# A two-layer decoder trunk: GpSimd takes over the low parts of the last three output-projection pieces, and the index mask is written in three steps

## The chip, the cores and the metric

The kernel runs on one core of one Trainium2 chip. The metric is the device time of one execution in microseconds (us), lower is better; the median of the runs is compared. Engines are named as the profile names them: PE is TensorE (matrix products), DVE is VectorE, ACT is ScalarE, POOL is GpSimd, SP is the engine that issues most transfers (DMA).

## What is computed

Two layers, each a token mixer and a mixture of experts, on 256 tokens of width 1024 in float32. The parts that matter here:

```python
p = _split_columns(x @ w_in)              # one input projection, 11 pieces of 256 columns
o_fox = _fox_attention(...)               # 4 heads
o_nsa = _nsa_attention(...)               # 6 heads: compressed + selected + window branches
o_dsa = _dsa_attention(...)               # 6 heads, keys picked by an index score:
#   score = where(pos_k <= pos_q, score, NEG); idx = top_k(score, 64)
o = jnp.concatenate([o_fox, o_nsa, o_dsa], axis=-1)
x = _layer_norm(ALPHA * x + o @ w_out)    # output projection, 4 pieces of 256 columns
x = _layer_norm(ALPHA * x + _moe(x))      # 64 experts, top 8, and one shared expert
```

## The kernel before, in words

Each engine has its own program, written out by hand, and the engines wait for each other on semaphores; what stands in one engine's program runs in that order. The two layers run the same code. Per layer there is an attention stage (some 160 us in layer 0, with the output projection, the layer norm and the routing) and an expert stage (some 460 us), in which the expert weights stream in.

**Weights in two parts.** Most products of the mixer are done three times, as high part by high part, low by high and high by low. A projection piece (128 partitions x 8 blocks x 256 columns, 2048 elements per partition) lies in one of five slots, `piece[n % 5]`. Its high part `piece_hi` is the piece rounded (`split_hi`, on ACT, L1244 to L1247; there are four slots for high parts). Its low part `piece_lo` is the piece minus its high part, written over the piece itself. Two engines share the low parts: the numbers in `LO_VECTOR` (L38) are done by DVE, with one instruction of 2048 elements (`split_lo`, L1634) or with two halves of 1024 (`split_out`, L1738); the others (`LO_POOL`) by POOL, with eight instructions of 256 elements (`split_lo`, L1488 to L1494). The pieces are numbered in the order in which they arrive: 9 to 12 are the last four input pieces, 13 to 16 the four output pieces.

**The attention units.** There are eleven units u = 0 to 10, two heads each (`UNITS`: fox 0 and 1, then selected and window alternating for u = 2 to 7, then dsa for 8 to 10). A unit goes through four engines: PE makes the scores (`scores(u)`); DVE takes the maxima (`maxima(u)`, L1668); ACT makes the exponentials (`exps(u)`, L1307); DVE divides by the sums (`normalise(u)`: a reciprocal L1678, for u = 2 to 7 a product with the gates L1681, two products over `prob` L1685); PE turns the result (`turn_probs`, L778); ACT copies it out (`probs_out`, L1325); PE multiplies it with the values (`add_values`, L802). The first five units are laid between the last input projection tiles (`project_tile`), with the rotation of the heads (`rotate`, L1560 to L1566) on DVE. The others run in a loop on each engine, in which PE does `scores(u + 2)`, `turn_probs` of u, and `add_values` of the turn before; DVE does `normalise(u)`, `maxima(u + 2)`; ACT does `exps(u + 1)`, `probs_out` of u and, for some, `heads_out` (L1317).

**The output projection.** It follows with 96 products. Its first parts are done early (`out_early`, between the last units): those need the low parts of pieces 13 and 14 and the first four heads in two parts (`heads_split` of 4). Those head parts, `x_hi` and `x_lo`, are made by POOL (L1509, L1510) for seven heads and by DVE (L1765, L1766) for the eighth, one head at a time as ACT delivers them. The next early part needs pieces 15 and 16.

**Index mask.** `index_top` marks the 64 best keys per query in `score` (128 x 384). `index_mask` (L1613) turns the marks into an additive mask `dmask` in bf16, which PE adds to the scores of the dsa units, 8 to 10.

SP's program issues the layer-norm rows, router and shared weights when the eighth head is out (`o_sb` of 8, L531 to L535), and the first expert weights when the output projection is nearly done (`mix`, L536).

## Time and profile before

| | us |
|---|---|
| median of 3 runs | 1241.99 (1241.19 to 1243.54) |
| profiled execution, whole time | 1243.89 |
| its span, first to last instruction | 1242.1 |
| PE busy | 1209.8 (97%) |
| DVE busy | 555.9 (45%) |
| ACT busy | 340.2 (27%) |
| POOL busy | 122.9 (10%) |

The page's chain that ended last goes through PE for 79% of the span, DVE 11%, DMA 6%, ACT 2%. Busy shares over the whole span say little about the attention stage, so that stage is read from the waits and the order of time. The two attention stages lie at 0 to 161 us and at 624 to 776 us. Where text below says layer 0 and layer 1, these are meant.

### The profile page before, as it was taken

Reading aid. Unit: us, or ns where it says so; the run is one execution under the profiler, and the core shown is the slowest. Engines: PE = TensorE matmul, PEld = TensorE weight load, DVE = VectorE, ACT = ScalarE, POOL = GpSimd, SP = SyncE. Lnnn points to the kernel's source line nnn. Section 1 sums busy time; section 2 is a strip of 40 time slices with the busy share of each in tenths; the row PEclk is TensorE's granted clock in tenths of the full one; section 3 lists DMA queues with packets and bytes.
Section 4 is the critical chain, followed back from the end, with each engine's and each line's share of the span. In section 5 each row is a group of like instructions: output and inputs, shape, how many; then the busy total and the mean of one; then the engine's idle time right before and its main releaser. Section 6 shows DMA issues by size and latency. Waiting matters only on the chain.

```text
span 1242.1 us, 25211 instructions
## 1 busy us (share of the span) xinstructions
PE 1209.8 (97%) x10381; PEld 631.4 (51%) x10383; DVE 555.9 (45%) x1550; ACT 340.2 (27%) x701; POOL 122.9 (10%) x173
## 2 busy tenths in 40 slices
PE   9998999999999999999999989999999999999995
PEld 7885754334344443433398858433433444443341
DVE  4788553333333333333468877433333333333334
ACT  4667321111111111111265574111111111111111
POOL 2662110000000000000035421000000000000000
PEclk9999999999999999999999999999999999999998
DMA  9444799999999999999945529999999999999994
GB/s 356 166 178 206 281 399 427 425 426 427 425 425 424 429 426 426 426 426 426 385 149 190 222 99 360 389 427 426 425 428 425 427 424 427 425 427 426 425 427 189
DMA packets 42425, 454.88 MB, mean 366 GB/s; under 512 B 4944, under 2 KB 5712, under 8 KB 8016
## 3 DMA queue, kind: packets, MB, share of 16 engines
q1 hardware_dynamic: 42032, 452.27, 87.6%
q8 instruction: 85, 1.39, 0.5%
q10 hardware_dynamic: 288, 1.05, 0.2%
q14 instruction: 20, 0.16, 0.0%
HBM read 452.26 MB, written 1.05 MB: 365 GB/s over the span
## 4 chain that ended last, share of the span: by engine, by line
PE 79%; DVE 11%; DMA 6%; ACT 2%; issue 2%; DVEq 0%; POOL 0%; ACTq 0%; POOLq 0%
PE banks L1050 33%; PE banks L1070 17%; PE banks L1026 7%; PE banks L1081 5%; DMA expert_weights<-in_moe_w 5%; PE banks L1058 2%; PE banks L970 1%; PE banks L917 1%; DVE prob L1685 1%; PE banks L918 1%; PE banks L919 1%; PE banks L633 1%; PE banks L1007 1%; PE banks L601 1%; DVE sm_neg L1668 1%
## 5 line engine op out<-in xcount | busy, mean ns | idle before, releaser
L1050 PE MATMUL banks<-expert_weights,gathered 128*64 128x512 f32 x1520 | 339.8, 595 | 1.4 <-DMA expert_weights<-in_moe_w 1.4
L1050 PEld LDWEIGHTS banks<-expert_weights,gathered 128*64 128x64 f32 x1520 | 105.6, 137 | 230.7 <-issue 230.7
L1070 PE MATMUL banks<-expert_weights,hT 128*32 128x512 f32 x1600 | 182.0, 595 | 2.5 <-DVE hT L1892 2.5
L1887 DVE TENSOR_TENSOR sig<-sig,banks 128x256 f32<-128x256 f32 x64 | 27.0, 421 | 338.9 <-ACT sig L1422 338.6
L1435 ACT ACTIVATE y_hi<-banks,gate_slot 128x512 fp32r<-128x512 f32 x126 | 86.6, 687 | 295.1 <-PE banks L1070 295.1
L1897 DVE SCALAR_TENSOR_TENSOR y_lo<-banks,gate_slot,y_hi 128x512 fp32r<-128x512 f32 x126 | 94.6, 751 | 157.4 <-ACT y_hi L1435 157.4
L1422 ACT ACTIVATE sig<-banks 128x256 f32<-128x256 f32 x64 | 24.6, 384 | 407.8 <-PE banks L1050 407.8
L1026 PEld LDWEIGHTS banks<-hot,x_part 128*128 128x128 bf16 x3072 | 93.3, 98 | 48.7 <-issue 48.7
L1070 PEld LDWEIGHTS banks<-expert_weights,hT 128*32 128x32 f32 x1600 | 47.2, 109 | 109.7 <-issue 108.2
L1026 PE MATMUL banks<-hot,x_part 128*128 128x64 bf16 x3072 | 100.7, 193 | 0.0
L1491 POOL TENSOR_TENSOR piece_lo<-piece,piece_hi 128x256 fp32r<-128x256 f32 x112 | 87.8, 819 | 80.3 <-ACT piece_hi L1247 65.2
L601 PE MATMUL banks<-piece_hi,x_hi 128*128 128x256 f32 x224 | 66.1, 295 | 0.0
L602 PE MATMUL banks<-piece_lo,x_hi 128*128 128x256 f32 x224 | 63.8, 285 | 0.0
L603 PE MATMUL banks<-piece_hi,x_lo 128*128 128x256 f32 x224 | 63.7, 285 | 0.0
L1050 PE MATMUL banks<-expert_weights_in_ring,gathered 128*64 128x512 f32 x256 | 58.1, 596 | 0.2 <-DMA expert_weights_in_ring<-in_moe_w 0.2
L1081 PE MATMUL banks<-y_hi,hotT 64*128 64x512 f32 x252 | 56.5, 444 | 0.1
L1247 ACT CAST piece_hi<-piece 128x2048 fp32r<-128x2048 f32 x24 | 45.6, 1903 | 22.2 <-DMA piece<-in_pieces 21.3
L1081 PE MATMUL banks<-y_lo,hotT 64*128 64x512 f32 x252 | 49.9, 391 | 0.0
L1873 DVE COPY gathered<-banks 128x512 f32<-128x512 f32 x64 | 44.3, 692 | 12.3 <-PE banks L1026 12.2
L1537 POOL TENSOR_TENSOR shared_hT<-shared_sig,shared_hT 128x512 f32<-128x512 f32 x2 | 2.6, 1282 | 477.0 <-ACT shared_hT L1444 477.0
L1426 ACT COPY gathered<-banks 128x512 f32<-128x512 f32 x64 | 37.5, 586 | 25.8 <-PE banks L1026 25.6
L601 PEld LDWEIGHTS banks<-piece_hi,x_hi 128*128 128x128 f32 x224 | 43.4, 194 | 1.1 <-issue 0.8
(244 smaller groups left out, 1526.0 us busy)
## 6 DMA issues: line engine op xcount, KB each, us to landing
expert_weights<-in_moe_w SPq DMA_DIRECT2D x132, 2048.0 KB, 23.2
expert_weights_in_ring<-in_moe_w SPq DMA_DIRECT2D x20, 2048.0 KB, 23.3
piece<-in_pieces SPq DMA_DIRECT2D x32, 1024.0 KB, 5.0
expert_weights<-in_moe_w SPq DMA_DIRECT2D x26, 1024.0 KB, 8.2
expert_weights_in_rows<-in_moe_w SPq DMA_DIRECT2D x22, 1024.0 KB, 22.5
expert_weights_in_x<-in_moe_w SPq DMA_DIRECT2D x22, 1024.0 KB, 23.3
expert_weights_in_ring<-in_moe_w SPq DMA_DIRECT2D x8, 1024.0 KB, 7.8
shared_weights<-in_ws SPq DMA_DIRECT2D x2, 3072.0 KB, 12.8
```

What stands on the lines that cost most here:

```text
L601: pe.matmul(out_, x_hi[:, k, cols], hi[:, k, :], start=(k == 0 and opens), stop=False, skip_group_check=True)
L602: pe.matmul(out_, x_hi[:, k, cols], lo[:, k, :], start=False, stop=False, skip_group_check=True)
L603: mm = pe.matmul(out_, x_lo[:, k, cols], hi[:, k, :], start=False, stop=(k == KD - 1), skip_group_check=True)
L1026: mm = pe.matmul(o[:, :, t, :], xs[j][t][:, d * P:(d + 1) * P], H[:, t, :, :], start=(j == 0), stop=(j == 2))
L1050: mm = pe.matmul(C[e * PAIR:(e + 1) * PAIR, :], xgT[:, d, e * PAIR:(e + 1) * PAIR], w[e][:, part], start=(d == 0), stop=(d == KD - 1))
L1070: mm = pe.matmul((A, B)[c][to:to + SLOTS, :], hT[:, f, of_:of_ + SLOTS], W[QUARTERS + c][e][:, f * 512:(f + 1) * 512], start=(f == 0), sto ...
L1081: mm = pe.matmul(bank[2 * t + c][:, :], hotT[par][rows_, :], y[rows_, c * 512:(c + 1) * 512], start=False, stop=False, skip_group_check=True)
L1247: act.copy(flat_piece(hi_of(n)), flat_piece(piece[n % RING])).then_inc(hi_ready, 1)
L1435: act.activation(y_hi[:, c * 512:(c + 1) * 512], (A, B)[c][:, :], ACT.Copy, scale=gslot[:, par:par + 1]).then_inc(sw.yh, 1)
L1491: own.mark(G.tensor_tensor(piece_lo[n % RING][:, k, :], piece[n % RING][:, k, :], hi_of(n)[:, k, :].bitcast(F32), ALU.subtract))
L1873: V.tensor_copy(xgT[:, 4:8, :], B[:, :].rearrange("p (k c) -> p k c", k=4)).then_inc(sw.xg_dve, 1)
L1897: V.scalar_tensor_tensor(y_lo[:, c * 512:(c + 1) * 512], (A, B)[c][:, :], gslot[:, par:par + 1], y_hi[:, c * 512:(c + 1) * 512].bitcast(F3 ...
```

## The change

It has three parts.

- **Low parts.** Pieces 14, 15 and 16 leave `LO_VECTOR`; DVE's `split_lo(14)` and its four halves `split_out` are gone. POOL makes them, after the compressed values (`vc_blocks`) and before the first head parts, eight instructions of 256 elements each.
- **High part of piece 16.** ACT's two half pieces (`split_last_hi`, L1249) are gone. POOL makes this one too, with eight copies of 256 elements, once the last input projection is done; `hi_ready` counts one less.
- **Index mask.** Before: one comparison over 384 columns, two additions of the causal mask over 128 columns, one cast over 384. Now: two comparisons over 128 columns in place, one that writes the middle 128 columns of `dmask` directly, and two minima of score and causal mask that write the outer 128 columns. `dmask_ready` counts to 3. Beside it, `masks_ready` takes the place of `heads_known` in layer 0.

```diff
-LO_VECTOR = (2, 3, 6, 14, 15, 16)
+LO_VECTOR = (2, 3, 6)
...
-        dmask_ready = sem("dsa_mask_ready", 1)
+        dmask_ready = sem("dsa_mask_ready", 3)
...
                     probs_out(4)
-                    split_last_hi(0)
                     read_turned(10)
...
                         heads_out(v - 1)
-                        if v == 6:
-                            split_last_hi(1)
...
                     if layer == 0:
-                        pool.wait_ge(heads_known, 1)
+                        pool.wait_ge(masks_ready, 1)
...
+                    for n in SPLIT_OUT[1:3]:
+                        rounded_by_scalar(n)
+                        split_lo(n)
+                    n = SPLIT_OUT[3]
+                    pool.wait_ge(*at(piece_ld[n % RING], piece_count(n)))
+                    hi_free(pool, n)
+                    for k in range(KD):
+                        own.mark(G.tensor_copy(hi_of(n)[:, k, :], piece[n % RING][:, k, :]))
+                    own.settle()
+                    split_lo(n)
                     pool.wait_ge(*at(proj, 2 * N_IN_PIECES))
                     pool.wait_ge(*at(m_ready, 6))
...
                     def index_mask():
-                        own.link(V.tensor_scalar(score[:, :], score[:, :], -2.0e38, NEG, ALU.is_gt, ALU.mult))
                         for a in (0, 2 * P):
-                            own.mark(V.tensor_tensor(score[:, a:a + P], score[:, a:a + P], cmask[:, 0, :], ALU.add))
+                            own.mark(V.tensor_scalar(score[:, a:a + P], score[:, a:a + P], -2.0e38, NEG, ALU.is_gt, ALU.mult))
+                        V.tensor_scalar(dmask[:, P:2 * P], score[:, P:2 * P], -2.0e38, NEG, ALU.is_gt, ALU.mult).then_inc(dmask_ready, 1)
                         own.settle()
-                        V.tensor_copy(dmask[:, :], score[:, :]).then_inc(dmask_ready, 1)
+                        for a in (0, 2 * P):
+                            V.tensor_tensor(dmask[:, a:a + P], score[:, a:a + P], cmask[:, 0, :], ALU.min).then_inc(dmask_ready, 1)
...
                     rotate(8)
                     index_mask()
-                    split_lo(14)
...
                         normalise(u)
-                        if 5 <= u < 9:
-                            split_out(2 + (u - 5) // 2, (u - 5) % 2)
-                        if u in (6, 8):
-                            own.settle()
-                            dve.nop().then_inc(lo_dve, 1)
```

POOL, from the low parts of pieces 12 and 13 to the first head, before (the number behind `piece_` is that of a slot: 57 holds piece 13, 58 piece 14, 54 piece 15, 55 piece 16):

```order
L1491 TENSOR_TENSOR piece_lo<-piece_56,piece_hi 128x256 x8
L1491 TENSOR_TENSOR piece_lo<-piece_57,piece_hi 128x256 x8
L1503 TENSOR_TENSOR vc_blocks<-vc_sb,own_head 96x384
L1509 CAST x_hi<-xT 128x256
L1510 TENSOR_TENSOR x_lo<-xT,x_hi 128x256
```

The same place of POOL after the change:

```order
L1477 TENSOR_TENSOR piece_lo<-piece_56,piece_hi 128x256 x8
L1477 TENSOR_TENSOR piece_lo<-piece_57,piece_hi 128x256 x8
L1494 TENSOR_TENSOR vc_blocks<-vc_sb,own_head 96x384
L1477 TENSOR_TENSOR piece_lo<-piece_58,piece_hi 128x256 x8
L1477 TENSOR_TENSOR piece_lo<-piece_54,piece_hi 128x256 x8
L1503 CAST piece_hi<-piece_55 128x256 x8
L1477 TENSOR_TENSOR piece_lo<-piece_55,piece_hi 128x256 x8
L1510 CAST x_hi<-xT 128x256
L1511 TENSOR_TENSOR x_lo<-xT,x_hi 128x256
```

Thirty-two instructions have come in between the compressed values and the first head.

DVE in the unit loop, units 5 and 6, before:

```order
L1678 RECIPROCAL sm_r<-sm_sum 128x4
L1681 TENSOR_TENSOR sm_r<-sm_r,gates 128x4
L1685 TENSOR_TENSOR prob<-prob,sm_r 128x2x128
L1685 TENSOR_TENSOR prob<-prob,sm_r 128x2x256
L1741 TENSOR_TENSOR piece_lo<-piece_54,piece_hi 128x1024
L1668 TENSOR_REDUCE sm_neg<-banks 128x2 x2
```

The same place of DVE after the change:

```order
L1680 RECIPROCAL sm_r<-sm_sum 128x4
L1683 TENSOR_TENSOR sm_r<-sm_r,gates 128x4
L1687 TENSOR_TENSOR prob<-prob,sm_r 128x2x128
L1687 TENSOR_TENSOR prob<-prob,sm_r 128x2x256
L1670 TENSOR_REDUCE sm_neg<-banks 128x2 x2
```

The half piece between the products over `prob` and the maxima has gone, in four units of each layer.

## Rows read from the trace of the kernel before

**Rows 1.** PE's waits, 64 to 135 us: us in total, times, longest
```profile
PE banks L778 <- DVEq L1687: 3.5, 4, 1.1
```

**Rows 2.** PE's waits, 679 to 750 us
```profile
PE banks L778 <- DVEq L1687: 3.6, 4, 1.3
```

**Rows 3.** PE in order of time: start, us, instruction, idle before and its releaser
```profile
89.07 0.44 PE L653 MATMUL banks<-ident,hq 128*128 128x128 f32 x2 [0.46 <-DVEq L1567]
...
120.15 0.84 PE L778 MATMUL banks<-ident,prob 128*128 128x128 f32 x6 [1.06 <-DVEq L1687]
...
703.06 0.69 PE L653 MATMUL banks<-ident,hq 128*128 128x128 f32 x2 [1.00 <-DVEq L1567]
...
735.56 0.85 PE L778 MATMUL banks<-ident,prob 128*128 128x128 f32 x6 [0.76 <-DVEq L1687]
```

**Rows 4.** Busy time by stretch: stretch, length, PE, PEld, DVE, ACT, POOL, PEclk, DMA, GB/s
```profile
702.60:706.10 3.50, 3.04 (x14) 2.96 (x14) 3.07 (x12) 2.79 (x8) 2.45 (x4) 0.51 1.03 433
```

**Rows 5.** DVE in order of time, the mask and piece 14, layer 0
```profile
79.28 0.67 DVE L1614 TENSOR_SCALAR score<-score 128x384 f32<-128x384 f32 x1
...
82.18 2.28 DVE L1636 TENSOR_TENSOR piece_lo<-piece,piece_hi 128x2048 fp32r<-128x2048 f32 x1
```

**Rows 6.** All instructions on tile piece_lo, two of its groups: ns min/median/max
```profile
L1491 POOL TENSOR_TENSOR piece_lo<-piece,piece_hi x112: 716/737/2828, 24.4 to 703.5; 128x256 fp32r<-128x256 f32 x112
...
L1741 DVE TENSOR_TENSOR piece_lo<-piece,piece_hi x8: 1224/1225/1528, 107.8 to 735.5; 128x1024 fp32r<-128x1024 f32 x8
```

**Rows 7.** POOL in order of time, layer 0, low parts of 12 and 13, then head parts
```profile
75.82 6.23 POOL L1491 TENSOR_TENSOR piece_lo<-piece,piece_hi 128x256 fp32r<-128x256 f32 x8 [8.23 <-DVEq L1687]
82.23 8.01 POOL L1491 TENSOR_TENSOR piece_lo<-piece,piece_hi 128x256 fp32r<-128x256 f32 x8 [0.18 <-POOL piece_lo L1491]
90.48 0.82 POOL L1503 TENSOR_TENSOR vc_blocks<-vc_sb,own_head 96x384 f32<-96x384 f32 x1 [0.24 <-POOL piece_lo L1491]
...
115.48 1.05 POOL L1510 TENSOR_TENSOR x_lo<-xT,x_hi 128x256 fp32r<-128x256 f32 x1
```

**Rows 8.** DVE, the same instructions with POOL idle and with POOL at work
```profile
74.66 1.02 DVE L1685 TENSOR_TENSOR prob<-prob,sm_r 128x256 f32<-128x256 f32 x2
...
101.63 0.17 DVE L1681 TENSOR_TENSOR sm_r<-sm_r,gates 128x4 f32<-128x4 f32 x1
...
106.13 0.45 DVE L1681 TENSOR_TENSOR sm_r<-sm_r,gates 128x4 f32<-128x4 f32 x1
...
680.14 1.94 DVE L1685 TENSOR_TENSOR prob<-prob,sm_r 128x256 f32<-128x256 f32 x2
```

**Rows 9.** DVE in order of time, from the compressed scores to unit 5, both layers
```profile
89.10 0.54 DVE L1720 TENSOR_TENSOR pc<-banks,misc_c 128x45 f32<-128x45 f32 x4
...
99.87 0.42 DVE L1560 TENSOR_TENSOR hq<-banks,rope_cs 128x256 f32<-128x256 f32 x1 [0.71 <-PE banks L603]
...
101.42 0.18 DVE L1678 RECIPROCAL sm_r<-sm_sum 128x4 f32<-128x4 f32 x1
...
103.00 2.19 DVE L1668 TENSOR_REDUCE sm_neg<-banks 128x2 f32<-128x256 f32 x4
...
707.46 1.02 DVE L1668 TENSOR_REDUCE sm_neg<-banks 128x2 f32<-128x256 f32 x2 [1.15 <-PE banks L760]
...
715.20 0.42 DVE L1560 TENSOR_TENSOR hq<-banks,rope_cs 128x256 f32<-128x256 f32 x1 [1.05 <-PE banks L603]
```

**Rows 10.** ACT in order of time: exponentials of unit 5, copy out, half piece
```profile
104.11 0.37 ACT L1307 ACTIVATE prob<-banks,sm_neg 128x128 f32<-128x128 f32 x1 [0.41 <-DVEq L1670]
...
106.01 0.80 ACT L1325 COPY probT<-banks 128x768 f32<-128x768 f32 x1 [0.17 <-ACT prob L1307]
...
110.34 1.04 ACT L1253 CAST piece_hi<-piece 128x1024 fp32r<-128x1024 f32 x1 [0.17 <-ACT probT L1325]
...
719.44 0.37 ACT L1307 ACTIVATE prob<-banks,sm_neg 128x128 f32<-128x128 f32 x1 [0.41 <-DVEq L1670]
```

**Rows 11.** The queue of SP: the first transfer after the attention units
```profile
130.44 0.33 SPq L532 DMA_DIRECT2D ln_rows<-in_lnw  x1
```

More of the change, by code:

```diff
@@ L1247, in split_hi @@
                         act.copy(flat_piece(hi_of(n)), flat_piece(piece[n % RING])).then_inc(hi_ready, 1)
-                    def split_last_hi(half):
-                        n, cols = SPLIT_OUT[3], slice(half * SLOT // 8, (half + 1) * SLOT // 8)
-                        act.wait_ge(*at(piece_ld[n % RING], piece_count(n)))
-                        hi_free(act, n)
-                        own.mark(act.copy(flat_piece(hi_of(n))[:, cols], flat_piece(piece[n % RING])[:, cols]))
-                        if half:
-                            own.settle()
-                            act.nop().then_inc(hi_ready, 1)
                     if layer == 0:
```

21 lines of the change are left out of this document (8 added, 13 removed).

## Prediction

> **What bounds the kernel now.** I looked for the stage in which DVE, ACT and POOL work can be on the path at all. The change touches only the attention stage, so I read PE's waits there first: between 64 and 135 us PE waits 3.5 us in four times for the end of `normalise` on DVE [rows 1], and in layer 1 3.6 us in four times [rows 2]. Beside these it waits once per layer for a rotated head, 0.46 us and 1.00 us [rows 3]. Where PE does not wait it is fed, so these waits are about all that a faster DVE can give back, unless the waits also change PE's clock.
>
> That they do, once: in layer 1, from 702.6 to 706.1 us, the granted clock is 0.51, so PE is at the lower of its two levels (1.2 GHz) [rows 4]; this begins in the 1.00 us for which PE stood idle before 703.06. In layer 0 the same place has an idle time of 0.46 us.
>
> After the attention units nothing else changes order, and later work hangs on their end: SP issues its first transfer after them at 130.44 us, when the eighth head is out [rows 11]. The expert stream starts behind that, so I pass on a shift of the attention stage one for one.
>
> **The change, part by part.**
>
> *Piece 14 and the mask.* DVE loses one instruction of 2.28 us at 82.18 [rows 5]. Behind it stand the rotation of a head and, at 89.10, the compressed scores [rows 9], for which DVE waits on PE. So only PE's 0.46 us (layer 0) and 1.00 us (layer 1) come back; the rest of the 2.28 us becomes idle time on DVE. In layer 1 the half-speed stretch should go too. The mask took 2.9 us from 79.28 to 82.18, with POOL at work [rows 5]: four instructions. Now it is five shorter ones, of which four or five meet POOL; I put it at 2.5 to 3.5 us. Since 2.28 us of idle time lie behind it and its reader is unit 8, some 30 us later, it costs nothing.
>
> *What POOL's work does to DVE.* This is the main term. POOL's instructions of 256 elements take 0.737 us in the median, but one took 2.828 us [rows 6], and one group of eight took 8.01 us instead of 6.23 [rows 7]: it stood beside DVE's 2.28 us instruction, so the two do not run at once. It goes the other way too: the pair of products over `prob` takes 1.02 us with POOL idle and 1.94 us with POOL at work, and the product with the gates 0.17 and 0.45 us [rows 8]. Each two-input DVE instruction waits for the running POOL instruction to end. That makes 0.92 + 0.28 = 1.2 us on a `normalise` of units 2 to 7, and 0.92 us on the others. Rotations, maxima and other reads of PSUM don't meet it.
>
> The Trainium skill says the same (GPSIMD Engine Reference, Key points): GpSimd shares its SBUF interfaces with VectorE, and contention is with instructions that have two SBUF inputs or run in a two-port mode. It speaks against this change, and the rows agree; it gives no price, and the sum goes by the rows.
>
> When does POOL now work? It ended `vc_blocks` at 91.3 us [rows 7]. Without DVE's 2.28 us lock-out this comes at about 89.4. Then two groups at 6.23 us, eight casts at about 0.4 each (my estimate, from half to all of the 0.737 us of a subtraction: 3 to 6 us), and a third group at 6.23: POOL is at work until about 112 us, where before it stood idle between 91.3 and the first head part, at about 104.
>
> *From 89 us to the exponentials of unit 5.* In this stretch DVE does `normalise` 2, 3 and 4, now each beside POOL: 3 x 1.2 = 3.6 us. One rotation and the four small products and subtractions of the compressed branch meet it also, at 0.1 to 0.45 us each; I take 1.0 together. Sum 4.6 us. Against it stands DVE's own idle time: in layer 0, 0.71 us [rows 9] and some 0.3 us in small waits, together 1.0, and the start that is 0.4 earlier (PE's wait gone). So unit 5's exponentials, which started at 104.11 on a wait for DVE [rows 10], come 4.6 - 1.0 - 0.4 = 3.2 us later. In layer 1 DVE idled 1.15 and 1.05 us [rows 9] and about 0.4 more, because PE ran slowly: 2.6 us, so 4.6 - 2.6 - 0.4 = 1.6 us later. PE's clock stretch and its 1.00 us are inside this, so they are not counted again.
>
> *From there to the turn of unit 8.* Before: from 104.11 to 120.15 [rows 3, 10] 16.04 us, and in layer 1 from 719.44 to 735.56 [rows 3, 10] 16.12 us. On DVE four half pieces go, 4 x 1.225 = 4.9 us and up to 5.2 with the slowest one [rows 6], and on ACT one half piece of 1.04 us [rows 10]; ACT's other one stood before a wait for DVE, and gives nothing. What is late next? DVE without them: 1.9 us of exponentials, four times 1.58 us of `normalise` (101.42 to 103.00 [rows 9]) and three times 1.17 us of maxima (1.02 and the step to the next), 11.7 us. ACT: exponentials 1.90 (104.11 to 106.01), copy 0.97 and a head copy 0.3 are some 3.1 us for each unit [rows 10]; three of them, then 1.9 and 1.6 us, are 12.8 us. So ACT's pace would hold, at 12.8. But POOL is still at work until 112, and then makes up for three heads: `normalise` 5 and 6 meet it fully and 7 in part, 2.4 to 3.6 us on DVE, 14.1 to 15.3 us. Some of it overlaps with ACT's pace; I take 14.5. The gain is 16.1 - 14.5 = 1.6 us in each layer.
>
> *Sum.* Layer 0: +3.2 - 1.6 = +1.6 us. Layer 1: +1.6 - 1.6 = 0. With 0.2 us for the casts that the last two units may still meet: **+1.8 us**. The profiled execution took 1243.89 us, 1.9 more than the median of 1241.99; a shift applies to both, so it would be 1245.7, and the median **1243.8 us**.
>
> **Ends of the range.** If POOL's work cost DVE nothing, unit 5 would come 0.5 us earlier in layer 0 and 2.3 in layer 1 (1.00 and some 1.3 us of slow clock), and the second stretch would be 12.8: -3.8 and -5.6, together -9.4 us, 1232.6. If every listed instruction paid the full 0.7 us of a POOL instruction, the first stretch would be some 2.4 us longer and the second 15.3: +3.2 us more in each layer, 1250.2. Both are further than the 8 in 10.
>
> **The rivals.**
>
> *Contention at half price (faster).* A DVE instruction is held only if it comes while a POOL instruction runs, and POOL may itself be held by DVE so often that both meet less. With 2.3 us in place of 4.6 in the first stretch and 13.5 in the second, layer 0 gives +0.9 - 2.6 = -1.7 and layer 1 -0.7 - 2.6 = -3.3: -5.0 us, 1237.0. For it: the product with the gates at 106.13 pays 0.28 us and not a whole POOL instruction of 0.737 [rows 6, 8]. Against it: where POOL works back to back, as now for over 20 us, the one pair in the trace paid in full. Chance 0.22.
>
> *The waits cost clock as well (slower).* PE's clock fell beside an idle time of 1.00 us. Now PE waits over 1 us for `normalise` 4, 5 and perhaps 6. Its idle times of up to 1.1 us in layer 0 [rows 1] did not bring the clock down, so this is open. One stretch like that of rows 4 costs some 1.3 us; one in each layer, on the forecast: +1.8 + 2.6 = +4.4 us, 1246.4. It decides from +0.7 us above the forecast on. The same sign comes if contention is a third above my price (+3 us). Chance 0.35.
>
> *POOL becomes the bound (slower).* It is done with piece 16 at about 112 us, then needs 1.2 to 1.7 us for each of four heads: 117 to 119. PE asks for the fourth head at about 122 to 124, so 3 us are left. Only with all three groups at 8.01 us would this be gone: then +1.8 and about 2 more, 1246. Chance 0.03, within the slower case.
>
> **How the numbers follow.** Forecast +1.8 us, within 0.2% (2.5 us, about what a measurement can tell from no change): 0.42. Half price or less: 0.22, which is faster. Slow clock, dearer contention or POOL as the bound: 0.36, slower. The range is 1237.5 to 1248.0: it takes in half price and one slow stretch in each layer with some contention above them. The likeliest case alone would be 1241.5 to 1245.
>
> **What would show it.** Right: `prob` pairs of units 2 to 5 at 1.7 to 1.95 us; POOL busy without a gap from 89 to 112 us; unit 5's exponentials near 107.3 in layer 0; the time from there to unit 8's turn near 14.5; no granted clock of 0.5 around 703 us. Wrong: pairs at 1.0 beside POOL (then it is faster), PE waiting for head parts L1511 or for the low parts of 15 and 16 before its early products (then POOL is the bound), or new half-speed stretches between 104 and 120 us.

## The result

The changed kernel takes 1248.60 us (median of five runs, 1246.85 to 1249.81), the kernel before, timed beside it, 1242.91 us: ratio 1.0046, 95% interval 1.0035 to 1.0057. It is 5.7 us slower, where +1.8 us was forecast, and lies 0.6 us above the range. Timed once more, beside new runs of the kernel before, the same kernel took 1247.46 us against 1242.25, ratio 1.0039 (1.0026 to 1.0052).

The profiled execution took 1248.61 us, with a span of 1246.7 us, 4.6 us more than that of before. Where they arise is read from three marks in each layer: the transfer of a piece by SP before the attention units, the first exponential of unit 5 on ACT, and SP's first transfer after the units. Three rows of SP's queue in the kernel after (both marks of layer 0, the last of layer 1), and two of ACT. The piece of layer 1 was issued at 683.74 us:

```profile
76.14 0.33 SPq L478 DMA_DIRECT2D piece<-in_pieces  x1
133.12 0.33 SPq L531 DMA_DIRECT2D ln_rows<-in_lnw  x1
...
750.81 0.33 SPq L531 DMA_DIRECT2D ln_rows<-in_lnw  x1
```
```profile
106.28 0.37 ACT L1297 ACTIVATE prob<-banks,sm_neg 128x128 f32<-128x128 f32 x1 [1.09 <-DVEq L1672]
...
723.86 0.37 ACT L1297 ACTIVATE prob<-banks,sm_neg 128x128 f32<-128x128 f32 x1 [1.09 <-DVEq L1672]
```

Before, the second and third mark of layer 0 stood at 104.11 and 130.44 us [rows 10, 11]; its piece was issued at 76.85. In layer 1 the three marks stood at 680.16, 719.44 and 745.85. I call the first stretch, from the piece to unit 5, part 1, and the second, from unit 5 to SP's transfer, part 2. All differences below are taken with these two parts, so that the chance shifts at the start of a run drop out:

| execution | part 1, layer 0 | part 2, layer 0 | part 1, layer 1 | part 2, layer 1 | PE at half speed in part 2 (layers 0, 1) |
|---|---|---|---|---|---|
| before | 27.26 | 26.32 | 39.28 | 26.41 | none (3.4 us in part 1 of layer 1) |
| after | 30.14 | 26.84 | 40.12 | 26.95 | 6.8, 6.8 us |
| after minus before | +2.9 | +0.5 | +0.8 | +0.5 | |
| forecast | +3.2 | -1.6 | +1.6 | -1.6 | |

Part 1 came out as worked out in layer 0, and below it in layer 1. The gain of part 2 is missing in both. The rest of the program moves by less than 1 us.

PE's waits between 64 and 135 us (us in total, times, longest), against [rows 1]: the waits for `normalise` are as long in total, but one of them is now 2.0 us, and those for ACT have grown from 1.2 to 2.3 us. The first two lines are of the kernel after, the third is of the kernel before.

```profile
PE banks L777 <- DVEq L1689: 3.4, 3, 2.0
PE banks L661 <- ACTq L1300: 2.3, 3, 1.3
```
```profile
PE banks L662 <- ACTq L1310: 1.2, 2, 0.8
```

In order of time, PE in both layers:

```profile
108.10 0.93 PE L661 MATMUL banks<-qkT 64*128 64x128 f32 x8 [1.34 <-ACTq L1300]
111.32 1.51 PE L777 MATMUL banks<-ident,prob 128*128 128x128 f32 x6 [1.97 <-DVEq L1689]
...
122.81 0.85 PE L777 MATMUL banks<-ident,prob 128*128 128x128 f32 x6
```
```profile
725.67 0.93 PE L661 MATMUL banks<-qkT 64*128 64x128 f32 x8 [1.34 <-ACTq L1300]
728.90 1.51 PE L777 MATMUL banks<-ident,prob 128*128 128x128 f32 x6 [1.98 <-DVEq L1689]
...
740.50 0.84 PE L777 MATMUL banks<-ident,prob 128*128 128x128 f32 x6
```

From unit 5's exponentials to the turn of unit 8 this is 16.53 us (122.81 less 106.28) and in layer 1 16.64, where the prediction had 14.5 and the kernel before 16.04 and 16.12.

The six transposes take 1.51 us behind the wait of 1.97 us and 0.85 us eleven microseconds later. The busy time by stretch (the columns of [rows 4]) says why: the granted clock is 0.51 for 6.9 us in each layer, so PE is at 1.2 GHz there. The stretch begins inside the wait, and in the 5.9 us before it (the third line, layer 0) the clock was at 1.00.

```profile
109.90:116.80 6.90, 5.48 (x26) 3.56 (x27) 4.92 (x9) 3.80 (x16) 4.12 (x7) 0.51 0.01 4
727.70:734.60 6.90, 5.70 (x27) 3.78 (x28) 4.92 (x8) 3.48 (x15) 3.90 (x7) 0.51 0.00 0
104.00:109.90 5.90, 4.01 (x32) 2.48 (x31) 4.82 (x9) 4.10 (x15) 5.82 (x9) 1.00 0.59 244
```

DVE in order of time, the `prob` products of units 2 to 6 and one subtraction of the compressed branch, and POOL from the low part of piece 14 on:

```profile
88.62 1.10 DVE L1726 TENSOR_TENSOR pc<-pc,pcs 128x90 f32<-128x90 f32 x2
...
90.37 2.08 DVE L1687 TENSOR_TENSOR prob<-prob,sm_r 128x256 f32<-128x256 f32 x2
...
96.23 2.04 DVE L1687 TENSOR_TENSOR prob<-prob,sm_r 128x256 f32<-128x256 f32 x2
...
103.69 1.33 DVE L1687 TENSOR_TENSOR prob<-prob,sm_r 128x256 f32<-128x256 f32 x2
...
109.08 2.04 DVE L1687 TENSOR_TENSOR prob<-prob,sm_r 128x256 f32<-128x256 f32 x2
```
```profile
88.17 6.24 POOL L1477 TENSOR_TENSOR piece_lo<-piece,piece_hi 128x256 fp32r<-128x256 f32 x8
94.59 6.46 POOL L1477 TENSOR_TENSOR piece_lo<-piece,piece_hi 128x256 fp32r<-128x256 f32 x8 [0.18 <-POOL piece_lo L1477]
101.28 3.19 POOL L1503 CAST piece_hi<-piece 128x256 fp32r<-128x256 f32 x8 [0.24 <-POOL piece_lo L1477]
104.56 6.01 POOL L1477 TENSOR_TENSOR piece_lo<-piece,piece_hi 128x256 fp32r<-128x256 f32 x8
110.83 0.55 POOL L1510 CAST x_hi<-xT 128x256 fp32r<-128x256 f32 x1 [0.26 <-POOL piece_lo L1477]
```

POOL is busy from 88 to 110.6 us, as worked out, and a pair of products costs 2.04 to 2.08 us beside its subtractions, a little above the 1.94 of [rows 8], and 1.33 beside its casts.

Behind unit 6 something else is new: DVE now waits for PE's scores before it can take the maxima, 1.62 and 0.90 us in layer 0 and 1.62 and 1.02 us in layer 1. Before, no maxima of this part waited over 0.3 us for them.

```profile
116.69 1.02 DVE L1670 TENSOR_REDUCE sm_neg<-banks 128x2 f32<-128x256 f32 x2 [1.62 <-PE banks L756]
...
120.20 1.02 DVE L1670 TENSOR_REDUCE sm_neg<-banks 128x2 f32<-128x256 f32 x2 [0.90 <-PE banks L756]
```

### The profile page after: what moved, and what is told of

Same layout as the page of the kernel before. It is cut to its first block, busy times and chain, and to the rows that moved or that the text cites. A ratio compares the mean times of both kernels' runs of the same rounds, so it can differ in the third digit from the quotient of the medians.

```text
span 1246.7 us, 25263 instructions
## 1 busy us (share of the span) xinstructions
PE 1212.5 (97%) x10383; PEld 633.4 (51%) x10383; DVE 554.3 (44%) x1542; ACT 336.3 (27%) x697; POOL 158.5 (13%) x237
## 3 DMA queue, kind: packets, MB, share of 16 engines
q10 hardware_dynamic: 288, 1.05, 0.2%
HBM read 452.26 MB, written 1.05 MB: 364 GB/s over the span
## 4 chain that ended last, share of the span: by engine, by line
PE 82%; DVE 9%; DMA 6%; ACT 1%; issue 1%; DVEq 0%; ACTq 0%
PE banks L1049 33%; PE banks L1069 17%; PE banks L1025 7%; PE banks L1080 5%; DMA expert_weights<-in_moe_w 5%; PE banks L1057 1%; PE banks L600 1%; PE banks L969 1%; PE banks L602 1%; PE banks L601 1%; PE banks L916 1%; DVE prob L1687 1%; PE banks L918 1%; PE banks L917 1%; PE banks L632 1%
## 5 line engine op out<-in xcount | busy, mean ns | idle before, releaser
L1477 POOL TENSOR_TENSOR piece_lo<-piece,piece_hi 128x256 fp32r<-128x256 f32 x160 | 120.4, 787 | 79.5 <-ACT piece_hi L1246 63.7
```

What stands on the lines that cost most here:

```text
L1477: own.mark(G.tensor_tensor(piece_lo[n % RING][:, k, :], piece[n % RING][:, k, :], hi_of(n)[:, k, :].bitcast(F32), ALU.subtract))
```

## The experiments

Each was timed in five rounds or more beside the kernel before on the same chip. Most changes are given against the kernel before or the changed one.

### The mask alone

```diff
-own.link(V.tensor_scalar(score[:, :], score[:, :], -2.0e38, NEG, ALU.is_gt, ALU.mult))
+for a in (0, 2 * P):
+    own.mark(V.tensor_scalar(score[:, a:a + P], score[:, a:a + P], -2.0e38, NEG, ALU.is_gt, ALU.mult))
...
-V.tensor_copy(dmask[:, :], score[:, :]).then_inc(dmask_ready, 1)
+for a in (0, 2 * P):
+    V.tensor_tensor(dmask[:, a:a + P], score[:, a:a + P], cmask[:, 0, :], ALU.min).then_inc(dmask_ready, 1)
```

> The kernel before with the new mask alone (two thresholds, one threshold straight into the mask tile, two minima). The theory of the prediction: the mask is hidden behind DVE's later wait for PE, so no change, within 0.6 us of before. A rival, in which the mask carries part of the 5.7 us by which the changed kernel is slower (a shift of DVE's work by 0.5 to 1 us that POOL then meets at other places): +1 to +3 us.

1243.16 us against 1243.10, ratio 1.0006 (0.9995 to 1.0018): no change. DVE in order of time, the first instruction of the mask and the one behind it:

```profile
78.81 1.23 DVE L1615 TENSOR_SCALAR score<-score 128x128 f32<-128x128 f32 x2
...
81.61 2.82 DVE L1637 TENSOR_TENSOR piece_lo<-piece,piece_hi 128x2048 fp32r<-128x2048 f32 x1
```

The mask takes 2.8 us, from 78.81 to 81.61, within the 2.5 to 3.5 us given for it. PE stood idle 0.98 us for the rotated head in layer 1, as before, and here no half-speed stretch followed: part 1 of layer 1 took 37.62 us in place of 39.28. So behind a wait of 1.0 us the clock falls in some executions and not in others. The two kernels also differ in the mask, so the 1.7 us are the most that this stretch can have cost.

### What could be gained at best

```diff
-LO_VECTOR = (2, 3, 6, 14, 15, 16)
+LO_VECTOR = (2, 3, 6)
...
-                    split_lo(14)
...
-                            split_out(2 + (u - 5) // 2, (u - 5) % 2)
...
-hi, lo = hi_ring[...], lo_ring[:, first % RING:first % RING + 2]
+hi, lo = hi_ring[...], hi_ring[:, hi_slot(first):hi_slot(first) + 2]
```

> The kernel before with the low parts of pieces 14, 15 and 16 left out: neither DVE nor POOL makes them, and the output projection takes the high parts in their place, with as many products. It has neither DVE's work nor POOL's, so it bounds what the move could give at best. The prediction's bound without contention was -9.4 us with the rounding of 16 off ACT too; here ACT keeps it, about 1 us a layer, so -7 us by that working, of which 1.3 us is a half-speed stretch that goes. Rival: PE's own pace or ACT's takes over sooner, -3 us. From here to the changed kernel is then the whole price of POOL's work: 13 us by the first, 9 us by the second.

The low parts of 14, 15 and 16 are left out. 1236.79 us against 1243.10, ratio 0.9951 (0.9938 to 0.9963): -6.3 us, close to the -7. This kernel computes less than the reference asks for; it is a bound and not a candidate. Parts 1 are 0.4 and 2.7 us shorter than before, parts 2 2.2 and 2.6 us. So layer 1 gains 5.3 us, near the 5.6 of the prediction's lower end, and layer 0 2.6 us where that had 3.8 (with the rounding off ACT too). From here to the changed kernel is the whole price of doing the work on POOL, what it does to PE included: 11 to 12 us.

### Piece 14 alone, and one instruction that is passed by six

```diff
-LO_VECTOR = (2, 3, 6, 14, 15, 16)
+LO_VECTOR = (2, 3, 6, 15, 16)
...
+split_lo(LO_POOL[-1])
...
-split_lo(14)
```

> The kernel before, of which only piece 14 goes from DVE to POOL; the low parts of 15 and 16 stay on DVE, the rounding of 16 on ACT, and the mask is the old one. Theory 1 (the clock makes the loss of the changed kernel): PE's waits stay short here, since POOL is done at about 96 us; no half-speed stretch in layer 0 and none around 703 us in layer 1; 0 to -3 us, and more if a stretch of layer 1 is gone. Theory 2 (contention makes it, evenly with POOL's work): a third of POOL's new work gives a third of the loss, about +2 us, less the 1.5 us of the two waits for a rotated head, so about +0.5 us, with the clock as before.

POOL makes piece 14 behind `vc_blocks`. 1247.84 us against 1243.10, ratio 1.0040 (1.0028 to 1.0052). Both expectations miss: a third of the work gives most of the loss. But the profiled execution took 1243.11 us, and the other five 1245.8 to 1249.4. I ran it again for another profile.

> The kernel with only piece 14 on GpSimd once more, unchanged, to have a profile of another execution and more times. Theory 1 (DVE is passed in some executions): the profile shows either about 1243 us and no DVE instruction held for over 1 us, or 1246 us and more and one that was held for 3 to 5 us, most likely one of the products or subtractions of the compressed branch beside piece 14. Theory 2 (instruction loading or the clock): a gap of 2 us and more on PE that waits for nothing, or half-speed stretches.

1249.14 us against 1242.11, ratio 1.0047 (1.0033 to 1.0061), and this profile caught what was missing. DVE, POOL and PE in the second profile, layer 0:

```profile
90.12 5.22 DVE L1725 TENSOR_TENSOR pc<-pc,pcs 128x90 f32<-128x90 f32 x2
```
```profile
89.68 5.56 POOL L1491 TENSOR_TENSOR piece_lo<-piece,piece_hi 128x256 fp32r<-128x256 f32 x8
```
```profile
97.14 1.51 PE L778 MATMUL banks<-ident,prob 128*128 128x128 f32 x6 [3.52 <-DVEq L1688]
```

In the first profile the same pair on DVE read:

```profile
89.13 1.10 DVE L1725 TENSOR_TENSOR pc<-pc,pcs 128x90 f32<-128x90 f32 x2
```

The first of the two subtractions took 4.53 us in place of 0.40. It came while POOL's first instruction on piece 14 ran, and was held through that and six more, which stand end to start behind it; POOL's group was not slowed at all (5.56 us for eight). The 3.52 us for which PE then waited were followed by a half-speed stretch of 6.8 us. Part 1 took 33.21 us in place of 28.30. Theory 1 holds in this profile. (Expectations further down speak of eight instructions: that is POOL's whole group. It is the running one and six that passed.)

The Trainium skill (SBUF — State Buffer, "SBUF: two separate sides") says that of two such instructions the one that starts first keeps the ports for its whole length and the other blocks. The holds of one instruction agree with it (the pair took 1.10 us beside POOL in the first profile, and 0.42 us without POOL in the run with piece 14 begun later, below); that the one that waits may be passed by six later ones is not in the rule, and is measured here.

Two edits test it. First, POOL waits for the end of each of its instructions on pieces 12 to 14 before it issues the next:

```diff
 for k in range(KD):
     own.mark(G.tensor_tensor(...))
+    if n >= 12:
+        own.settle()
```

> The kernel with only piece 14 on GpSimd, with the same edit. That kernel's profiled execution took 1243.1 us, its other ones 1245.8 to 1249.4. Theory 1: what they have more is DVE passed by many GpSimd instructions, 3 to 5 us in one place; with the instructions apart all runs come to 1240 to 1244 us. Theory 2: the times stay at 1246 to 1249 us.

1243.65 us against 1242.11, ratio 1.0009 (1.0000 to 1.0018); eleven of twelve runs lie between 1242.8 and 1244.6. The 5 us are gone although POOL's group now takes 7.05 us. Second, the instructions end to start as they were, but begun only after DVE's subtraction:

```diff
+pool.wait_ge(*at(sc_sub, 1))
 split_lo(LO_POOL[-1])
```

> The kernel with only piece 14 on GpSimd, its eight instructions end to start as there, but begun only when DVE's subtraction in the compressed branch is done. In three kernels whose profile showed it, or didn't, the +5 us stood with that subtraction: passed by eight instructions in one execution (1249.0 us) and not in another (1243.1). Theory 1 (it is this meeting): no passing there, median 1242 to 1244.5 us in place of 1247.8 to 1249.1, without a gap between GpSimd's instructions. Theory 2 (any DVE instruction meets the same chance in a back-to-back group): passed elsewhere, median at 1246 us and more.

1243.14 us against 1242.25, ratio 1.0005 (0.9995 to 1.0015). DVE and POOL:

```profile
89.59 0.42 DVE L1726 TENSOR_TENSOR pc<-pc,pcs 128x90 f32<-128x90 f32 x2
```
```profile
90.14 6.38 POOL L1491 TENSOR_TENSOR piece_lo<-piece,piece_hi 128x256 fp32r<-128x256 f32 x8 [0.96 <-DVEq L1728]
```

So it is this one meeting: in this profile the other DVE instructions beside the same back-to-back group are held, but not passed. The edit with gaps in the kernel before, whose POOL groups are those of 12 and 13:

> The kernel before with the same edit: GpSimd's instructions on pieces 12 and 13 one at a time. The runs of the kernel before spread over 5 us (1240.4 to 1245.9). Theory 1 (in some executions DVE is passed by many GpSimd instructions): the slowest runs go, the median falls by 1 to 2 us. Theory 2 (the spread has another cause): the median and the spread stay.

1244.29 us against 1242.11, ratio 1.0012 (1.0003 to 1.0021): slightly slower, and the spread stays. Theory 1 falls for the kernel before. Its spread has another cause, which I did not find. The profile of this run has a wait of 1.70 us for the rotated head of layer 1 in place of 1.00.

### How long one hold is

```diff
-own.mark(G.tensor_tensor(piece_lo[n % RING][:, k, :], ...))
+for a in (0, P) if n >= 12 else (0,):
+    cols = slice(a, a + P) if n >= 12 else slice(0, PIECE)
+    own.mark(G.tensor_tensor(piece_lo[n % RING][:, k, cols], ...))
+    if n >= 12:
+        own.settle()
```

> The kernel with only piece 14 on GpSimd, its instructions apart, and each of them on 128 elements of a row in place of 256 (16 for a piece, pieces 12 to 14). If a DVE instruction is held until the running GpSimd instruction ends, halved ones hold it half as long: the pairs beside them fall from about 1.9 us to about 1.4, and the time by 0 to 1 us from 1243.65 (more instructions on GpSimd, each with its own start, take part of it back: a piece takes 8 us in place of 6.6). If the hold is a fixed price of each meeting: pairs as before, and up to 1 us slower.

This is the kernel with piece 14 alone, with 16 instructions of 128 elements in a piece in place of 8 of 256, one at a time. 1243.40 us, ratio 1.0017 (1.0008 to 1.0026), where the one with 8 had 1.0009 (1.0000 to 1.0018): no gain in time. But the two pairs beside POOL read, in DVE's order of time:

```profile
90.06 1.44 DVE L1690 TENSOR_TENSOR prob<-prob,sm_r 128x256 f32<-128x256 f32 x2
...
95.38 1.43 DVE L1690 TENSOR_TENSOR prob<-prob,sm_r 128x256 f32<-128x256 f32 x2
```

A pair takes 1.02 us with POOL idle [rows 8], 2.04 to 2.08 beside instructions of 256 elements end to start, and 1.57 beside the same ones apart, where only its second product is held, by 0.53 us. Here both are held, by 0.15 and 0.26 us. So a hold shortens with the POOL instruction: it is the rest of the running one and not a fixed price. But there are more of them, and with 0.1 us off a pair nothing comes out in the time.

### PE's clock in the changed kernel

```diff
+if v == 6:
+    pe.wait_ge(*at(o_sb, 2))
+    for _ in range(8):
+        pe.matmul(bank[7][:, 0:T], still[:, 0:P], still[:, 0:T], start=True, stop=True, ...)
 if what == "unit" and u + 2 < NU:
     scores(u + 2)
...
+if v in (6, 7):
+    pe.wait_ge(*at(pt_sb, v))
+    for _ in range(12 if v == 6 else 5):
+        pe.matmul(bank[5][:, 0:T], ...)
 turn_probs(v)
```

> The changed kernel, with 25 extra products of 128x256 bf16 zeros in each layer that PE makes where it otherwise stands idle around 105 to 115 us: 8 before the scores of unit 7, 12 before the turn of unit 6 and 5 before the one of unit 7. All other work and its order are those of the changed kernel. Theory 1 (half-speed stretches make the loss): both stretches of 6.8 us are gone or shorter, and the time falls by 3 to 5 us from the changed kernel's +5.7 us, to +1 to +2.5 us. Theory 2 (contention alone makes it; PE at half speed is only hidden beside waits): the stretches go, and the time stays at +5 to +6 us.

1250.45 us against 1243.10, ratio 1.0058 (1.0045 to 1.0071). The stretches are gone, and by the time alone theory 2 would stand. The profile says that the time of this run doesn't decide it, because two other things came in. Stretches, then two rows of DVE, then PE between the layers:

```profile
109.90:116.80 6.90, 5.74 (x50) 3.88 (x49) 6.21 (x12) 4.41 (x18) 4.32 (x7) 1.00 0.00 1
727.70:734.60 6.90, 5.66 (x50) 3.85 (x49) 5.79 (x10) 5.29 (x21) 6.40 (x11) 1.00 0.01 2
```
```profile
119.08 1.02 DVE L1678 TENSOR_REDUCE sm_neg<-banks 128x2 f32<-128x256 f32 x2 [1.05 <-PE banks L756]
...
706.38 5.21 DVE L1734 TENSOR_TENSOR pc<-pc,pcs 128x90 f32<-128x90 f32 x2
```
```profile
621.16 1.04 PE L821 MATMUL banks<-still 128*128 128x512 bf16 x4 [2.18 <-issue]
```

The pair of subtractions took 5.21 us in layer 1, passed as above, and PE waited 3.5 us for it. And the program, longer by 50 products, has a gap of 2.18 us on PE in which nothing that the profile shows is waited for. In part 2, where the clock was kept, it did gain: 25.54 and 25.53 us in place of 26.84 and 26.95, that is 1.3 and 1.4 us. Most of it is the wait of 1.62 us for PE's scores, which is gone; the next, for unit 9, is still 1.05 us, at full clock. From unit 5's exponentials to the turn of unit 8 it takes 15.23 us in both layers, so 0.7 us above the forecast of 14.5 stay with the clock kept.

The same with the gaps on POOL, and with 13 products of 512 columns:

```diff
+for _ in range(4):
+    pe.matmul(bank[7][:, 0:2 * T], still[:, 0:P], still[:, 0:2 * T], ...)
...
+for _ in range(6 if v == 6 else 3):
+    pe.matmul(bank[5][:, 0:2 * T], still[:, 0:P], still[:, 0:2 * T], ...)
...
+if n >= 12:
+    own.settle()
```

> The changed kernel with GpSimd's instructions one at a time, and with 13 extra products of 128x512 bf16 zeros in each layer in PE's waits around 105 to 115 us (half as many, twice as long as in the first such kernel). Theory 1 (two causes that add: passing, and half-speed stretches): both stretches go, and 1245.5 falls by 1.3 us for the one stretch that its profile had, to 1244 us; with the same gap in PE's instruction supply as the first one had (2.2 us near 619 us) 1246.5. Theory 2 (clock doesn't matter): 1245 to 1246 us without such a gap.

1244.17 us against 1241.73, ratio 1.0018 (1.0009 to 1.0027), as theory 1 had it, with parts 2 of 24.92 and 24.93 us, no stretch, and no such gap on PE. Only the gaps on POOL, the changed kernel otherwise:

```diff
+if n >= 12:
+    own.settle()
```

> The changed kernel, in which GpSimd waits for the end of each of its instructions on the low parts of pieces 12 to 16 before it issues the next, so that they no longer stand end to start. In the trace of the run with kept clock DVE's subtraction in the compressed branch was passed by six GpSimd instructions in a row (4.5 us instead of 0.46). Theory 1 (part of the loss is DVE that doesn't get its turn between back-to-back GpSimd instructions): no DVE instruction is held for more than one GpSimd instruction, the pairs over the probabilities fall from 1.94 to 2.08 us to under 1.8, and the time falls by 1 to 4 us from the changed kernel's. Theory 2 (each DVE instruction waits for one GpSimd instruction either way, and GpSimd's work only gets longer, by 8 times about 0.1 us in each group): same time or up to 2 us slower.

1245.48 us against 1242.11, ratio 1.0023 (1.0012 to 1.0035): about half of the loss is gone. Against it the extra products of the run just told gain 0.6 to 0.9 us (by the ratios, by the medians), and the two intervals overlap; so no time on record shows the clock's price by itself, and what follows about it is read from profiles. DVE and PE:

```profile
108.76 1.56 DVE L1689 TENSOR_TENSOR prob<-prob,sm_r 128x256 f32<-128x256 f32 x2
...
112.57 1.56 DVE L1689 TENSOR_TENSOR prob<-prob,sm_r 128x256 f32<-128x256 f32 x2
```
```profile
108.30 1.65 PE L661 MATMUL banks<-qkT 64*128 64x128 f32 x8 [1.59 <-ACTq L1300]
```

The pairs of units 5 and 6 are held once and not twice. This profile has one stretch of 6.8 us, in layer 0, from 108.04 us: it begins in the wait of 1.59 us for ACT, and the turn of unit 5 then follows at 110.52 us without any idle time before it. In layer 1 the same wait for ACT was followed by none.

The changed kernel itself once more gave a second measure of the clock:

> The changed kernel once more, unchanged, for a profile of another execution. Theory 1 (two half-speed stretches and one-for-one holds make its loss; passing is a matter of chance in it): median 1248 to 1249 us, both stretches again beginning in PE's wait of about 2 us for the normalisation of unit 5; an execution above 1249.5 us has a DVE instruction that was passed by several of GpSimd's. Theory 2 (its one profile was an odd one): another pattern, with passing and without the stretches.

1247.46 us. PE and the stretches in this second profile:

```profile
111.79 1.51 PE L777 MATMUL banks<-ident,prob 128*128 128x128 f32 x6 [1.98 <-DVEq L1689]
```
```profile
111.80:115.20 3.40, 3.40 (x18) 2.36 (x20) 3.19 (x6) 1.69 (x6) 2.95 (x6) 0.50 0.00 0
729.60:733.00 3.40, 3.40 (x19) 2.04 (x16) 2.78 (x6) 2.14 (x9) 1.84 (x3) 0.50 0.00 0
```

The same kernel and the same wait of 1.98 us, but the stretch is 3.4 us and not 6.8. Parts 2 took 25.86 and 25.87 us instead of 26.84 and 26.95. So the 3.4 us of half speed that this profile has less are worth 1.0 to 1.1 us, with no edit between. Against the run with the clock kept, 6.8 us cost 1.3 to 1.4, so that leaves 0.3 us for the other 3.4. No instruction was passed in either profile.

Part 2 by the half-speed time in it, from the profiles (some of these kernels are told further down). The first eight rows are changed kernels, the others still have DVE's half pieces, but for the last. Five more profiles of kernels with the half pieces have no stretch in part 2, and parts 2 of 26.3 to 26.5 us.

| kernel | layer 0: half speed, part 2 | layer 1: half speed, part 2 |
|---|---|---|
| changed, first profile | 6.8, 26.84 | 6.8, 26.95 |
| changed, second profile | 3.4, 25.86 | 3.4, 25.87 |
| changed, extra products | none, 25.54 | none, 25.53 |
| changed, POOL's instructions apart | 6.8, 25.88 | none, 24.95 |
| the same with extra products | none, 24.92 | none, 24.93 |
| changed, POOL's instructions on 15 and 16 apart | none, 25.10 | 3.4, 25.30 |
| changed, piece 14 on DVE | none, 25.16 | 3.4, 25.89 |
| changed, piece 14 begun later | none, 24.26 | none, 24.30 |
| before | none, 26.32 | none, 26.41 |
| before, piece 14 on POOL and begun later | 3.4, 26.33 | none, 26.42 |
| before, piece 14 in halves | 3.4, 26.29 | none, 26.38 |
| before, pieces 12 and 13 apart | none, 26.34 | 3.4, 26.25 |
| before, rounding of 16 on POOL | none, 26.35 | 3.4, 26.21 |
| before, low parts left out | none, 24.08 | none, 23.80 |

Two things stand in this table. First, a stretch of 3.4 us costs nothing where DVE still makes its half pieces: four profiles have one in part 2, and it is as long as without. In the changed kernels 6.8 us cost 1.3 to 1.4 us, and 0.9 with POOL's instructions apart. Second, three of these four stand behind waits that the kernel before has too, the longest of them 0.8 us. One of them, in the kernel with piece 14 on POOL and begun later, begins at 108.51 us (first two lines); the third line is the same turn in the kernel before, where no stretch follows:

```profile
108.34 1.37 PE L778 MATMUL banks<-ident,prob 128*128 128x128 f32 x6 [0.66 <-DVEq L1689]
```
```profile
108.50:111.90 3.40, 3.40 (x20) 2.36 (x21) 3.19 (x7) 3.04 (x8) 1.62 (x2) 0.50 0.06 19
```
```profile
107.85 0.85 PE L778 MATMUL banks<-ident,prob 128*128 128x128 f32 x6 [0.67 <-DVEq L1687]
```

So the length of the one wait before it does not decide whether a stretch comes.

### Which group, and which meeting

The changed kernel with DVE making piece 14 as before:

```diff
-LO_VECTOR = (2, 3, 6)
+LO_VECTOR = (2, 3, 6, 14)
```

> The changed kernel, in which DVE makes the low part of piece 14 as before; pieces 15 and 16 and the rounding of 16 stay on GpSimd, back to back. GpSimd is then done with about 6 us less work, at about 106 to 107 us, and the subtraction of the compressed branch (the instruction that was passed by eight in two profiles) comes before GpSimd's first subtraction on 15. Theory 1 (GpSimd's amount of work beside the normalisations sets the loss, and passing comes with piece 14): 1243 to 1245.5 us, 3 to 5 below the changed kernel. Theory 2 (the loss sits in the second part of the stage, from unit 5 on, where 16 is made): 1247 us and more.

1246.65 us against 1241.73, ratio 1.0038 (1.0024 to 1.0052), between both expectations. Parts 2 are 25.16 and 25.89 us, but a half-speed stretch now stood in part 1 of layer 0 (at 89.5 us, behind a wait of 1.04 us for the rotated head) and one at 727.8. In layer 0 PE waited 1.78 us for unit 5's `normalise`, and no stretch followed. The edit did not do what was expected of it: POOL waited 2.6 us for the rounding of 15 and 3.2 us for PE's last projection, and ended piece 16 at 112.2 us and not at 106 to 107, so the run does not separate the two theories.

The changed kernel, with piece 14 begun only after the subtraction:

> The changed kernel, in which GpSimd begins piece 14 only when DVE's subtraction in the compressed branch is done; all else, back-to-back groups too, as in the changed kernel. Theory 1 (in the changed kernel the loss stands in the second part, from unit 5 on, and that meeting costs it nothing in most executions): 1247 to 1249 us, as the changed kernel. Theory 2 (being passed there is in its median too): 1243 to 1245.5 us.

1244.74 us against 1242.74, ratio 1.0019 (1.0010 to 1.0028), so theory 1 as I wrote it falls: the place of the first group matters to the changed kernel too. But not by passing. Against the changed kernel POOL starts 1.0 us later on piece 14 (from the piece's transfer on), its groups meet the normalisations otherwise, and PE's wait is shorter:

```profile
108.30 0.93 PE L661 MATMUL banks<-qkT 64*128 64x128 f32 x8 [1.59 <-ACTq L1300]
110.99 0.85 PE L777 MATMUL banks<-ident,prob 128*128 128x128 f32 x6 [1.44 <-DVEq L1690]
```
```profile
109.00:120.00 11.00, 9.26 (x77) 5.58 (x74) 9.79 (x19) 8.69 (x32) 8.98 (x13) 1.00 0.02 5
724.00:735.00 11.00, 9.25 (x75) 5.71 (x76) 9.48 (x19) 8.70 (x34) 8.46 (x12) 1.00 0.01 1
```

The wait was 1.44 us, no stretch followed in this execution (1242.50 us), and parts 2 took 24.26 and 24.30 us: 2.1 us less than before, more than the 1.6 forecast. Of its twelve executions, three had a mean clock of 0.997 or 0.998 and took 1242.5, 1242.9 and 1243.4 us; the nine with 0.992 to 0.995 took 1243.7 to 1248.0, 1245.4 on average. These 2.4 us are no pure price of the clock: whatever makes PE wait longer in an execution lengthens it and lowers the clock as well. In the three executions that kept it, the moved work costs nothing against the kernel before, and gains nothing.

The gaps on the groups of 15 and 16 alone:

```diff
+if n >= 15:
+    own.settle()
```

> The changed kernel with GpSimd's instructions one at a time on pieces 15 and 16 alone; 12, 13 and 14 stay back to back. With all five apart it came to 1245.5 us. Theory 1 (the gain of that comes from unit 5 on, where the normalisations of units 5 and 6 and piece 16 meet): 1245 to 1246.5 us, with at most one half-speed stretch in a layer. Theory 2 (it came from the groups before): 1247 us and more.

1244.22 us, ratio 1.0014 (1.0005 to 1.0023), 1 us below the expectation. Parts 2 are 25.10 and 25.30 us. So either edit, at the first group or at the last two, takes about 3 us away. No run has both; the one with all five groups apart is no faster than this one. What both do is to shorten the wait of 2.0 us in part 2 (here 1.2 us).

### The rounding alone, and piece 14 on DVE in halves

```diff
-                    split_last_hi(0)
...
-                            split_last_hi(1)
...
+for k in range(KD):
+    own.mark(G.tensor_copy(hi_of(n)[:, k, :], piece[n % RING][:, k, :]))
```

> The kernel before, of which only the rounding of piece 16 goes from ScalarE to GpSimd (eight casts after the compressed values); DVE makes all three low parts as before, with the old mask. ScalarE loses two instructions of 1.04 us in each layer, of which one stood before a wait for DVE. If the half piece at 110.34 was on the path: -1 us in each layer, 1240 to 1241 us. If DVE's pace holds there, with its four half pieces: no change, within 0.6 us, or +0.5 us for the casts beside one normalisation.

1242.40 us against 1241.73, ratio 1.0010 (1.0001 to 1.0019): no gain. Parts 2 are 26.35 and 26.21 us, as before. ACT's half pieces were not on the path by themselves.

```diff
-split_lo(14)
+split_14(0)
 rotate(9, (0,))
+split_14(1)
...
```

> The kernel before, with piece 14 made by DVE in two halves, one before the first half of the ninth head's rotation and one behind it, where the profile without these pieces shows 1.3 us of idle time on DVE. GpSimd and the mask are as before. It tells what the move of piece 14 could give without GpSimd: 0.46 us in layer 0, and in layer 1 1.0 us and the half-speed stretch (1.3 us) where that stood: -0.5 to -2.5 us, 1240 to 1241.5 us. Rival: the second half only moves the wait to the maxima of unit 2 and from there to PE, no change.

1244.73 us against 1242.25, ratio 1.0020 (1.0010 to 1.0029): slower. PE waited 1.59 us for the rotated head of layer 1 in place of 1.00, since the second half went ahead of its second rotation, and a stretch followed; another stands in part 2 of layer 0. The wait, then both stretches:

```profile
704.54 0.44 PE L653 MATMUL banks<-ident,hq 128*128 128x128 f32 x2 [1.59 <-DVEq L1567]
```
```profile
108.30:111.70 3.40, 3.40 (x20) 2.36 (x22) 3.19 (x7) 3.05 (x8) 1.67 (x2) 0.50 0.04 14
705.60:709.00 3.40, 3.40 (x18) 2.46 (x17) 2.06 (x6) 2.14 (x2) 0.41 (x1) 0.50 1.05 443
```

My reading of that idle time as room for half a piece was wrong. No complete version tried beats the kernel before.

## Why the prediction was wrong

- **What bounds the kernel; a shift of the attention stage passes on one for one:** right. SP's transfer came 2.7 us later than before, in layer 1 5.0 us, and the span ended 4.6 us later.
- **The mask costs nothing:** right, by the first experiment.
- **Piece 14 gives back 0.46 and 1.00 us and layer 1's stretch:** right in the sum. Parts 1 came out at +2.9 and +0.8 us where +3.2 and +1.6 were worked out. That the stretch of layer 1 goes was luck in part: the kernel with the mask alone lost it too, with the same wait.
- **Contention at 0.92 us a pair, POOL busy from 89 to 112 us, POOL not the bound:** right in size and place: 2.04 to 2.08 us a pair, 88 to 111 us. In part 2 units 5 and 6 paid 1.6 and 1.2 us, products with the gates included, 2.8 where 2.4 to 3.6 had been counted. The prediction says that rotations don't meet POOL; their last product does, 0.82 us in place of 0.43 (piece 14 begun later, 102.28 us). The halved instructions show that the mechanism is the one named. What I did not foresee is that a DVE instruction can be passed by six; it sets the loss of the kernel with piece 14 alone, but stands in neither profile of the changed kernel, so I can't give it a share there.
- **Part 2 gains 1.6 us in each layer:** this is the step that failed. The stretch from unit 5's exponentials to the turn of unit 8 was put at 14.5 us and took 16.53 and 16.64; part 2 came out at +0.5 us, 2.1 too high in each layer and 4.3 together. Part 1 gave 1.1 of it back, and the median missed by 3.9. The sum asked which of DVE and ACT sets the pace, and took PE as always ready and at full clock. DVE's own terms and the contention in it were right; what it left out is that DVE, without its half pieces, waits for PE's scores: 2.5 us in layer 0 and 2.6 in layer 1. Of the 2.1 us, 1.3 to 1.4 are PE's clock, by the run with extra products. The other 0.7 to 0.8 stay with the clock kept, and there DVE still waits 1.05 us for PE. That these make the 0.7 to 0.8 is my reading of the trace; no run takes that wait away alone. Where POOL's groups meet the normalisations otherwise, part 2 does gain 1.4 to 1.5 us (gaps and extra products) and 2.1 us (piece 14 begun later), so the forecast of 1.6 was not out of reach.
- **The rival "the waits cost clock as well"** is what happened in the larger part, and its mechanism, place ("new half-speed stretches between 104 and 120 us") and sign were right. Its price of 1.3 us in each layer is what the run with extra products gives, but that is luck: it was taken from one stretch of 3.4 us, and it bought 6.8 here. With it the rival read +4.4, the profiled span grew by 4.6, and the median by 5.7. Its chance of 0.35 was too low by the prediction's own terms: PE waited 0.67 us before the turn of unit 5 in the trace of before (the line at 107.85 us above), and 1.2 us more on that `normalise` makes 1.9 us; it came out at 1.97.

What stays open: what decides whether the clock falls behind a wait, and for 3.4 or 6.8 us; which of the changed kernel's runs have an instruction passed; why one back-to-back meeting is passed and others are not; and the spread of the kernel before.

## What to carry to other kernels

Before work is moved off an engine, ask what sets the pace once it is gone, the busiest engine included. Here VectorE's half pieces had hidden TensorE's pace: half-speed stretches of 3.4 us cost nothing beside them, and without them VectorE waited 2.5 us for TensorE in this part, and 6.8 us at half speed cost 1.3 to 1.4 us in each layer. Work given to GpSimd beside VectorE's two-input instructions is worth trying with a gap between its instructions, and with its start behind a VectorE instruction on the critical chain and not just before it; moving the start by 1.0 us, or spacing the last two groups, took back about 3 of 5 us here. Shorter instructions made the holds shorter, but not the time. And when one profile of a kernel disagrees with its median, take another profile before explaining either.

## What the runs showed of the hardware

- A two-input DVE instruction waits for the running GpSimd instruction to end, and in some executions for the next six as well: 4.53 us in place of 0.40, seen in two profiles at the same instruction, and in none of the four profiles in which GpSimd's instructions stood 0.08 us apart there.
- The same wait of 1.98 us was followed by 3.4 us of half speed in one execution and 6.8 us in another; waits of 1.59 us by 6.8 us, 3.4 us or nothing; one of 1.0 us or of 0.66 us by 3.4 us or nothing; one of 1.44 us and one of 1.78 us by nothing.
- 6.8 us of half speed cost 0.9 to 1.4 us in part 2 of the changed kernels, and 3.4 us less of it gave back 1.0 to 1.1; 3.4 us cost nothing in four profiles of kernels in which DVE still makes its half pieces.
- With 50 more PE instructions in the program PE had a gap of 2.18 us 619 us into the run, with no semaphore behind it; with 26 more it had none. Each is one profile, and the cause of the gap is not shown.
